# The first two units of a decoder step begin side by side, chunk by chunk, from nine transfers

## The reference

```python
def rmsnorm(x, g):
    xf = x.astype(F32)
    y = xf * lax.rsqrt(jnp.mean(xf * xf, axis=-1, keepdims=True) + EPS)
    return (y * g.astype(F32)).astype(x.dtype)

def swiglu(h, w_in, w_out):
    gu = h @ w_in
    g, u = jnp.split(gu, 2, axis=-1)
    return (jax.nn.silu(g) * u) @ w_out
...
    x = x + 0.5 * swiglu(rmsnorm(x, g_norm[l, 0]), w_ffn_in[l, 0], w_ffn_out[l, 0])
```

## Time and profile before

| | |
|---|---|
| median of 3 runs | 1241.29 us (1241.18 to 1241.52) |
| profiled execution, its own time | 1241.22 us |
| span of its profile, first to last instruction | 1239.4 us |
| TensorE busy | 1233.5 us |
| VectorE busy | 726.1 us |
| ScalarE busy | 583.0 us |
| GpSimd busy | 81.1 us |
| loaded from memory | 193.03 MB |

### The profile page before, as it was taken

One profiled execution on the slowest core, in us unless ns is written; L12 is line 12 of the kernel. 1 busy time (PEld: TensorE's weight loads), 2 busy tenths in 40 slices (PEclk: granted clock), 3 DMA queues, 4 the chain that ended last, 5 costly groups with the idle time before them and its releaser, 6 DMA issues.

```text
span 1239.4 us, 22055 instructions
## 1 busy us (share of the span) xinstructions
PE 1233.5 (100%) x8875; PEld 1209.5 (98%) x8875; DVE 726.1 (59%) x1127; ACT 583.0 (47%) x936; POOL 81.1 (7%) x99
## 2 busy tenths in 40 slices
PE   9999999999999999999999999999999999999998
PEld 8999999989999999999998999999998999999998
DVE  6656554575777656554564565655467485565433
ACT  6534333464557444443445554533345474444343
POOL 0000000100322000000000000000020110000010
PEclk9999999999999999999999999999999999999999
DMA  9343334543354443334544734334578734433341
GB/s 341 137 164 141 115 129 157 206 146 130 125 164 153 152 166 135 137 118 142 191 159 140 259 135 159 135 114 144 167 280 319 275 141 140 165 135 127 122 159 43
DMA packets 34778, 200.39 MB, mean 162 GB/s; under 512 B 4050, under 2 KB 4186, under 8 KB 19490
## 3 DMA queue, kind: packets, MB, share of 16 engines
q1 hardware_dynamic: 32706, 192.24, 44.3%
q0 software_dynamic: 2016, 7.39, 1.9%
HBM read 193.03 MB, written 6.57 MB: 161 GB/s over the span
## 4 chain that ended last, share of the span: by engine, by line
PE 99%; DMA 0%; DVE 0%; SPq 0%; issue 0%; ACT 0%; DVEq 0%
PE bank L552 30%; PE bank L554 30%; PE bank L553 29%; PE bank L710 1%; PE bank L709 1%; PE bank L708 1%; PE bank L1050 1%; PE bank L712 1%; PE bank L711 1%; DMA xp<-xp_in 0%; PE bank L863 0%; PE bank L818 0%; PE bank L966 0%; PE bank L992 0%; PE bank L956 0%; PE bank L948 0%
## 5 line engine op out<-in xcount | busy, mean ns | idle before, releaser
L552 PE MATMUL bank<-h_hi,w_hi 128*128 128x320 f32 x1792 | 555.6, 310 | 0.6 <-DVE h_lo L1673 0.6
L554 PE MATMUL bank<-h_hi,w_lo 128*128 128x320 f32 x1792 | 553.7, 309 | 0.0
L553 PE MATMUL bank<-h_lo,w_hi 128*128 128x320 f32 x1792 | 553.7, 309 | 0.0
L1213 ACT ACTIVATE w_hi<-raw 128x1024 fp32r<-128x1024 f32 (+1 forms) x364 | 331.9, 958 | 441.2 <-PE bank L554 422.2
L1659 DVE TENSOR_TENSOR w_lo<-raw,w_hi 128x1024 fp32r<-128x1024 f32 (+1 forms) x364 | 388.4, 1107 | 133.4 <-ACT w_hi L1213 133.4
L552 PEld LDWEIGHTS bank<-h_hi,w_hi 128*128 128x128 f32 x1792 | 336.4, 188 | 2.9 <-issue 1.3
L553 PEld LDWEIGHTS bank<-h_lo,w_hi 128*128 128x128 f32 x1792 | 336.5, 188 | 0.1
L554 PEld LDWEIGHTS bank<-h_hi,w_lo 128*128 128x128 f32 x1792 | 336.5, 188 | 0.0
L553 PE MATMUL bank<-f_lo,w_hi 128*128 128x320 f32 x704 | 216.5, 308 | 0.0
L552 PE MATMUL bank<-f_hi,w_hi 128*128 128x320 f32 x704 | 216.5, 308 | 0.0
L554 PE MATMUL bank<-f_hi,w_lo 128*128 128x320 f32 x704 | 216.5, 308 | 0.0
(11 more groups left out here) (263 smaller groups left out, 761.5 us busy)
## 6 DMA issues: line engine op xcount, KB each, us to landing
raw<-w_in SPq DMA_DIRECT2D x86, 1024.0 KB, 4.8
raw<-w_out SPq DMA_DIRECT2D x64, 704.0 KB, 4.1
raw<-w_a SPq DMA_DIRECT2D x12, 1024.0 KB, 4.8
raw<-w_kv SPq DMA_DIRECT2D x8, 1024.0 KB, 4.7
raw<-w_oa SPq DMA_DIRECT2D x4, 1024.0 KB, 5.6
raw<-w_q SPq DMA_DIRECT2D x4, 1024.0 KB, 4.8
raw<-w_ob SPq DMA_DIRECT2D x4, 1024.0 KB, 11.9
raw<-kc_in SPq DMA_DIRECT2D x8, 512.0 KB, 4.5
```

The lines of the kernel that those rows point to most:

```text
L552: pe.matmul(out, wh, mh, start=first, stop=False)
L553: pe.matmul(out, wh, ml, start=False, stop=False)
L554: return pe.matmul(out, wl, mh, start=False, stop=last)
L1213: sc.activation(w_hi[:, n_at % 2, part * w:part * w + w], raw[:, raw_of(n_at) % RAW, part * w:part * w + w], ACT.Copy).then_inc(hi_done, 1)
```

## The change

Units 0 and 1 are now loaded and multiplied side by side. The three groups of chunks are (0, 1), (1, 4) and (4, 8), that is 1, 3 and 4 chunks. For each group SP issues three transfers, x, unit 0 and unit 1, so nine in place of six and two. ScalarE and VectorE work chunk by chunk (one instruction for each chunk of each unit) and treat unit 1 one chunk behind unit 0. TensorE does the same. Of warm-up matmuls there are seven in one go, in place of nine, two and one. Unit 2 takes over unit 1's loading in halves; it uses slot 0 of `w_hi`, and so waits for unit 0's end. Unit 3 gets banks 6 and 7 and is written out ahead of the loop. On ScalarE the squares go ahead of unit 2's copies, and split 4 goes ahead of hidden 0; on VectorE split 4 goes ahead of hidden 0 and scaled 2 behind it, split 5 ahead of hidden 2, and scaled 3 behind that.

```diff
-PIECES = ((0, 2), (2, 5), (5, 8))
+PIECES = ((0, 1), (1, 4), (4, 8))
...
+            def first_loads():
+                last = len(PIECES) - 1
+                for q, (a, e) in enumerate(PIECES):
+                    c = slice(P_COLS + T * a if q else 0, P_COLS + T * e)
+                    sp.dma_start(xp[:, c], xp_in[:, c]).then_inc(s_x[q], 16)
+                    w = slice(256 * a, 256 * e)
+                    sp.dma_start(raw[:, 0, w], w_in[0, 0][:, w]).then_inc(w0_piece[q] if q < last else loaded[0], 16)
+                    sp.dma_start(raw[:, 1, w], w_in[0, 1][:, w]).then_inc(w1_piece[q] if q < last else loaded[1], 16)
...
-                zeros(9)
-                pe.wait_ge(lo_piece, 1)
-                zeros(2)
-                pe.wait_ge(s_x[0], 16)
-                zeros(1)
...
+                zeros(7)
+                pe.wait_ge(w0_hi, 1)
+                pe.wait_ge(hh_done, 1)
+                begin()
+                second_unit(0)
+                first_unit(1)
+                for kt in range(2, KT):
+                    mm = first_unit(kt)
+                    if kt == KT - 1:
+                        mm.then_inc(unit_done, 1)
+                    second_unit(kt - 1)
+                second_unit(KT - 1).then_inc(unit_done, 1)
                 pe.wait_ge(lo_first, 1)
-                chunk(bank[2][:, 0:T], 1, 0)
-                pe.wait_ge(lo_done, 2)
-                chunk(bank[3][:, 0:T], 1, 1).then_inc(unit_done, 1)
-                pe.wait_ge(lo_first, 2)
                 for kt in range(KT):
                     if kt == 5:
                         total(0)
                     chunk_part(bank[4][:, 0:T], 0, 0, kt)
                 pe.wait_ge(lo_done, 3)
                 chunk(bank[5][:, 0:T], 0, 1).then_inc(unit_done, 1)
+                pe.wait_ge(lo_done, 4)
+                pe.wait_ge(root_done, 1)
+                chunk(bank[6][:, 0:T], 1, 0)
+                chunk(bank[7][:, 0:T], 1, 1).then_inc(unit_done, 1)
...
+            first_hi(0)
+            second_hi(0)
+            first_hi(1)
+            for k in range(2, KT):
+                first_hi(k)
+                second_hi(k - 1)
+            second_hi(KT - 1)
             sc.wait_ge(s_set, 4)
 
             def first_post():
-                half = PAIR // 2
-                sc.wait_ge(w1_half, 16)
-                sc.activation(w_hi[:, 1, 0:half], raw[:, 1, 0:half], ACT.Copy).then_inc(hi_done, 1)
-                sc.wait_ge(loaded[1], 16)
-                sc.activation(w_hi[:, 1, half:PAIR], raw[:, 1, half:PAIR], ACT.Copy).then_inc(hi_done, 1)
                 for i in range(2):
                     sc.activation(sq_room[:, 4 * i:4 * i + 4, :], x[:, 4 * i:4 * i + 4, :], ACT.Square
                                   ).then_inc(sq_first, 1)
-                split_at(2)
+                half = PAIR // 2
+                sc.wait_ge(w2_half, 16)
+                sc.wait_ge(unit_done, 1)
+                sc.activation(w_hi[:, 0, 0:half], raw[:, 2, 0:half], ACT.Copy).then_inc(hi_done, 1)
+                sc.wait_ge(loaded[2], 16)
+                sc.activation(w_hi[:, 0, half:PAIR], raw[:, 2, half:PAIR], ACT.Copy).then_inc(hi_done, 1)
                 split_at(3)
                 root_of(0)
+                split_at(4)
                 hidden(0, 0, 0)
                 hidden(0, 1, 1)
-                split_at(4)
+                split_at(5)
                 hidden(0, 2, 2)
-                split_at(5)
                 hidden(0, 3, 3)
...
                 split_at(3)
                 rms_of(0)
                 scaled(0, 0, 0, 0)
                 scaled(0, 1, 1, 0)
+                split_at(4)
                 hidden(0, 0, 0)
+                ve.wait_ge(hid_lo, 1)
+                scaled(0, 2, 2, 0)
                 hidden(0, 1, 1)
-                for k in (2, 3):
-                    scaled(0, k, k, 0)
-                    split_at(k + 2)
-                    hidden(0, k, k)
+                split_at(5)
+                hidden(0, 2, 2)
+                scaled(0, 3, 3, 0)
+                hidden(0, 3, 3)
```

More of the change, by code:

```diff
@@ L640, in first_units, with begin @@
-                mm.then_inc(unit_done, 1)
+                def begin():
+                    w = [slice(c * KT * 128, c * KT * 128 + 128) for c in range(2)]
+                    for c in range(2):
+                        pe.matmul(bank[c][:, 0:T], w_hi[:, 0, w[c]], h_hi[:, 0, :], start=True, stop=False)
+                    pe.wait_ge(hl_done, 1)
+                    for c in range(2):
+                        pe.matmul(bank[c][:, 0:T], w_hi[:, 0, w[c]], h_lo[:, 0, :], start=False, stop=False)
+                    pe.wait_ge(w0_lo, 1)
+                    for c in range(2):
+                        pe.matmul(bank[c][:, 0:T], w_lo[:, 0, w[c]], h_hi[:, 0, :], start=False, stop=False)
@@ new lines, in both, with first_unit, second_unit @@
+                def both(u, kt):
+                    for c in range(2):
+                        mm = chunk_part(bank[2 * u + c][:, 0:T], u, c, kt)
+                    return mm
+                def first_unit(kt):
+                    pe.wait_ge(hl_done, kt + 1)
+                    if kt < KT - 1:
+                        pe.wait_ge(w0_lo, kt + 1)
+                    else:
+                        pe.wait_ge(lo_done, 1)
+                    return both(0, kt)
+                def second_unit(kt):
+                    if kt < KT - 1:
+                        pe.wait_ge(w1_lo, kt + 1)
+                    else:
+                        pe.wait_ge(lo_done, 2)
+                    return both(1, kt)
@@ L1766, in first_post, with first_lo @@
[L1766 to L1772 removed]
+            piece_of = [q for q, (a, e) in enumerate(PIECES) for k in range(a, e)]
+            def first_lo(k):
+                h_lo_of(k, N_A0, k + 1)
+                if k < KT - 1:
+                    ve.wait_ge(w0_hi, k + 1)
+                else:
+                    ve.wait_ge(hi_done, 2)
+                ve.tensor_tensor(piece(w_lo, 0, k, k + 1), raw_piece(0, piece_of[k], k, k + 1),
+                                 piece(w_hi, 0, k, k + 1).bitcast(f32), ALU.subtract
+                                 ).then_inc(w0_lo if k < KT - 1 else lo_done, 1)
@@ new lines, in second_lo @@
+            def second_lo(k):
+                if k < KT - 1:
+                    ve.wait_ge(w1_hi, k + 1)
+                else:
+                    ve.wait_ge(hi_done, 4)
+                ve.tensor_tensor(piece(w_lo, 1, k, k + 1), raw_piece(1, piece_of[k], k, k + 1),
+                                 piece(w_hi, 1, k, k + 1).bitcast(f32), ALU.subtract
+                                 ).then_inc(w1_lo if k < KT - 1 else lo_done, 1)
+            first_lo(0)
+            second_lo(0)
+            first_lo(1)
@@ L1776, in first_post @@
                 ve.tensor_tensor(sqsum[:, :], sq_room[:, 0, :], sq_room[:, 1, :], ALU.add).then_inc(sum_first, 1)
+                split_half(2, 2, 1)
                 split_at(3)
```

110 lines of the change are left out of this document (57 added, 53 removed).

## The result

The changed kernel takes 1244.54 us in the median of 11 executions (1242.90 to 1245.16 us) against 1241.30 us before (1240.83 to 1242.76 us): 3.2 us more, ratio 1.0023 with a 95% interval of 1.0015 to 1.0031. I had said 1241.6 us, and 1242.8 us as the upper end.

The account below looks back on a forecast made before the run. TensorE was taken to bound the kernel, so only unit 2's start counted: -0.7 us (twelve passes done earlier), +1.0 us (wait before unit 2), 0 behind: +0.3 us, 1241.6 us. The main case spans 1241.1 to 1242.3 us; upper end 1242.8 us.

Parts of the forecast that it names:

- What bounds the kernel: Whole run: TensorE is busy 1233.5 of 1239.4 us, so the whole prize lies ahead of 9.10 us.
- unit 0's chunks 1 to 3 (1317 KB) by 6.37 + 320/480 x 1.33 = 7.26 us: Start: landing of unit 0's second group, interpolated on the earlier kernel's curve of bytes against time.
- T: Start of TensorE's thirteenth pass, unit 0's chunk 1: forecast 8.4 us against 9.10 us before, 0.7 us won.
- the half microsecond that I had named as a sign of being wrong: Start: the prediction counts as wrong if the thirteenth pass's start is off by over half a microsecond.
- rival B: Start: two additional small transfers each hold the queue 0.47 us, the group lands 0.9 us later, 1242.5 us; chance 0.10.
- Chunk 0: Start: real passes begin at about 4.95 us, 1.8 us earlier; both units' twelve passes finish by about 6.8 us.
- The wait before unit 2: Unit 2's split waits for unit 0's slot, stalling TensorE 1.0 us, bounds 0.8 to 1.15 us.
- Rival D: Start: fewer warm-up matmuls make TensorE's clock rise later, costing only behind 8.4 us; chance 0.06, half beyond 0.2%.
- a gap of 1.4 us: Start: TensorE's wait for w_lo of unit 0's chunk 1, about 1.4 us, ending near 8.4 us.
- Behind unit 2: After unit 2's start: other waits cost nothing; unit 4 is tightest with 0.2 us to spare, bound 0.5 us.
- rival C: Unit 4: a table switch costing 1.38 us more makes unit 4 start 1.2 us late, 1242.8 us; chance 0.05.
- main case: Whole run: T between 8.1 and 8.8 us, stall 0.8 to 1.15 us, up to 0.5 us at unit 4; chance 0.64.

Follow-up runs that it names:

- f4_groups_only: Kernel before with only the change's groups of 1, 3 and 4 chunks, nothing side by side; 1242.91 us.
- g2_split_first: Kernel before with its first group of two chunks cut into two groups of one, nothing side by side; 1243.02 us.
- f1_joint: Changed kernel with fillers (three and six matmuls on zeros), unit 0's last chunk moved earlier, and both units' weights in one transfer for the first two groups; 1245.12 us.
- e3_fill_tail: Changed kernel with matmuls on zeros in both gaps and, on TensorE, unit 0's last chunk ahead of unit 1's chunk 5; 1241.88 us.
- e1_fill: Changed kernel with three matmuls on zeros ahead of unit 1's chunk 0 and eight ahead of unit 0's chunk 1; 1242.63 us.
- g3_half_fill: Changed kernel with four matmuls on zeros in the long gap alone, none in the short one; 1243.16 us.
- g1_by_group: Changed kernel with the groups of before (2, 3, 3 chunks) and unit 1 a whole group behind unit 0 on all three engines; 1240.92 us.
- e4_four_groups: Changed kernel with four groups of chunks (1, 1, 2, 4), twelve transfers instead of nine; 1245.03 us.
- e2_tail: Changed kernel with unit 0's last chunk ahead of unit 1's chunk 5 on TensorE, no fillers; 1244.45 us.

## Why the prediction was wrong

**What bounds the kernel.** Right. Everything happened ahead of unit 2; behind it both spans are the same to 0.1 us.

**The step that failed: "unit 0's chunks 1 to 3 (1317 KB) by 6.37 + 320/480 x 1.33 = 7.26 us".** It landed at 8.6 us. I laid the new transfers on the old curve of bytes against time, as if the curve belonged to the chip. It belongs to those six transfers. With first groups of one chunk the queue moved 237 to 283 GB/s from 2 to 9 us instead of 340 (f4_groups_only and g2_split_first show it without anything side by side), and the landing came 1.4 us behind the count of bytes instead of 0.8 to 0.9 us. So T was 9.68 us, not 8.4 us: 1.3 us of the miss, and more than the half microsecond that I had named as a sign of being wrong. What follows the landing took 1.02 us, as reckoned (1.1 us). My rival B had the sign, but 0.9 us for it, a time of 1242.5 us and a chance of 0.10. Its mechanism, a hold of 0.47 us for each additional transfer, isn't shown: f1_joint has two transfers fewer and moved the same 272 GB/s. The last group of unit 0 was late too (ScalarE waited for it until 12.69 us, where I had a landing at 11.2 us), which no wait of TensorE shows.

**Chunk 0.** Real passes began at 4.22 us (4.95 us said), because the first landing was earlier than reckoned: ScalarE's copy of w_hi began at 3.76 us and not at 4.36 us, and the hand-over took 0.06 us instead of 0.15 us. Unit 1's chunk 0 came at 6.33 us; on the prediction's terms it was 5.8 us (4.95 and six passes), right behind unit 0's. Neither moved T, but the wait of 0.89 us between them wasn't in the prediction, and it is part of the idle time ahead of the clock's fall.

**The wait before unit 2.** Right in place, kind and size: 0.94 us by starts of passes, which is how I had reckoned the 1.0 us, and within its bounds. ScalarE began at 22.14 us and the next 2.45 us are its half, VectorE's half and the hand-over. e3_fill_tail removes it.

**The clock.** Here the reasoning failed, not just a size. Rival D asked when the clock *rises*, and said that the new gap hides a late rise. It rose in time, and *fell* again behind that gap and the one before it, when TensorE had been back at work for 1.5 us; filling both kept it (e1_fill). I had noted a gap of 1.4 us at this place and gave it no price: the fall of the clock is a term that the sum leaves out. The gap was 2.2 us long, because of the first error, and the fall cost 1.6 us. With the landing as reckoned the clock might have held, as it mostly did with 0.46 and 1.25 us (g3_half_fill), but that isn't shown. Of the clock at the start, one reading was indirect: the granted clock of the earlier trace rows is 1.00 from 1.20 to 4.50 us, so the lower level there is argued from the 0.22 us between matmuls, and the row doesn't confirm it. By the same sign the rise comes at different times: the changed kernel's passes are 0.15 us apart from 4.69 us on, those of e3_fill_tail still 0.27 us apart from 4.92 to 5.99 us, where its granted clock reads 1.00 too.

**Behind unit 2.** Costed at nothing, and nothing it was: no wait of TensorE at unit 4, so rival C is out. The table load took 1.28 us and the silu began 1.30 us after the load's start. The drain that the Trainium skill gives in ScalarE: Activation LUTs, "What ACT_TABLE_LOAD costs", is not seen here either.

**Sum.** Said +0.3 us; the misses are +1.3 (T), -0.1 (wait), +1.6 (clock), +0.35 (outside the span) and +0.1 us (behind unit 2), together 3.55 us, as between the two profiled executions; between the medians it is 3.2 us. The range had a slip of its own: T at 8.8 us, a stall of 1.15 us and 0.5 us at unit 4 add up to 1242.65 us, not to the 1242.3 us given for the main case.

## What to carry to other kernels

A curve of landings read from one order of transfers doesn't hold for another: cutting the very first transfers smaller to start earlier can make the second group come later by more than it gains. Price each idle stretch of TensorE twice, once for its length and once for the clock it may lose afterwards. Useless matmuls as a filler cost nothing as long as they end before the data is ready; in e3_fill_tail they ran 0.4 us past it. When two units share the start, let the second follow a whole group behind, so that in no engine's program it stands ahead of work that has landed: here some 1.4 us better than chunk by chunk with the same groups, though not shown to beat one unit after the other.

## What the runs showed of the hardware that I had not expected

- TensorE's granted clock fell to half for 3.4 us after two idle stretches of 0.89 and 2.22 us, while TensorE was at work again. In g1_by_group it fell at 7.5 us after 1.25 us of idle at the start and 0.32 us more, but in f4_groups_only it stayed at 1.00 after 2.54 us. The length of an idle stretch alone doesn't tell. Half clock meant a pass each 0.27 us instead of 0.146 us.
- The loading queue's rate from 2 to 9 us depends on how it begins: 304 to 340 GB/s in the four kernels whose first two transfers are of 256 and 357 KB, 237 to 283 GB/s in the nine that begin with 128 and 197 KB, and 272 GB/s in f1_joint, which begins with 197 and 256 KB. Every kernel has microseconds between 2 and 9 us with only 100 to 290 GB/s (two before the change, seven in e4_four_groups), and their place moves with the order. What the queue does in them remains open: f1_joint excludes the number of transfers alone, and the size of the rows, the size of the transfers and the first access to each region weren't told apart.
- A landing follows the count of moved bytes by a time that varies: 0.8 to 0.9 us before the change, 1.4 us in the changed kernel and 2.2 us in e2_tail for the same group, at nearly the same rate (272 and 270 GB/s). The average rate of a queue doesn't give the landing of one transfer.
- The time outside the span goes with the program: 1.82 us in the profiled execution before, and in the median 1.81 and 1.82 us in f4_groups_only and g2_split_first, but 2.12 to 2.16 us in the changed kernel and all ten made from it. These 0.3 us are a tenth of the change's cost, and why they come is open.
